# Token pairs interleaved in the stationary tiles, and weight columns streamed and written backward, in a hybrid decoder layer

## What is computed

```python
h = _rms_norm(x, attn_norm_g[l])
proj = h @ w_in[l]
...
merged = (jax.nn.sigmoid(g_da) * (o_da @ w_o_da[l])
          + jax.nn.sigmoid(g_ret) * (o_ret @ w_o_ret[l])
          + jax.nn.sigmoid(g_mem) * (o_mem @ w_o_mem[l]))
x = x + merged @ w_out[l]
hf = _rms_norm(x, ffn_norm_g[l])
x = x + (jax.nn.silu(hf @ w_ffn_gate[l]) * (hf @ w_ffn_up[l])) @ w_ffn_down[l]
```

## Time and profile before

| | |
|---|---|
| median of the runs | 1623.02 us |
| profiled execution | 1622.59 us, its span 1620.8 us |
| TensorE: matmuls | 7355, busy 1613.9 us |
| TensorE: loads of stationary values | 7355, busy 1336.1 us |
| VectorE | busy 1305.7 us |
| ScalarE | busy 915.7 us |
| GpSimd | busy 80.6 us |
| memory traffic | 341 MB, mean 211 GB/s |

### The profile page before, as it was taken

The page is one execution under the profiler, slowest core; times in us unless marked ns, Lnnn a source line. Parts: engine busy times, 40 slices in busy tenths (PEclk is TensorE's granted clock), DMA queues, the critical chain, the costliest instruction groups (busy, mean ns, idle before and its releaser), DMA issues.

```text
span 1620.8 us, 19825 instructions
## 1 busy us (share of the span) xinstructions
PE 1613.9 (100%) x7355; PEld 1336.1 (82%) x7355; DVE 1305.7 (81%) x1361; ACT 915.7 (56%) x993; POOL 80.6 (5%) x73
## 2 busy tenths in 40 slices
PE   9999999999999999999999999999999999999999
PEld 7888888888888888888888888888888888888887
DVE  5565658898677777787975589999999999999995
ACT  6654555555555544444554455665656655656653
POOL 0000000000011000000000000100100100100101
PEclk9999999999999999999999999999999999999999
DMA  9776555666645555566666746868868868868866
GB/s 351 268 214 194 157 150 177 213 201 196 193 156 168 165 162 172 180 186 202 206 233 192 258 147 210 256 211 254 243 216 245 252 206 251 246 217 240 251 213 177
DMA packets 178013, 341.45 MB, mean 211 GB/s; under 512 B 11792, under 2 KB 16400, under 8 KB 177168
## 3 DMA queue, kind: packets, MB, share of 16 engines
q1 hardware_dynamic: 167056, 319.45, 60.8%
q0 software_dynamic: 10880, 20.97, 7.1%
HBM read 317.31 MB, written 2.10 MB: 197 GB/s over the span
## 4 chain that ended last, share of the span: by engine, by line
PE 85%; issue 11%; DVE 1%; POOL 1%; DMA 1%; ACT 0%; DVEq 0%; ACTq 0%; SPq 0%; POOLq 0%
PE acc L1600 38%; PE at L1692 9%; PE at L1691 9%; PE at L1690 9%; PE acc L1692 5%; PE acc L1690 5%; PE acc L1691 5%; PE at L1600 3%; PE at L1622 2%; POOL rstd L487 1%; PE at L1653 0%; PE at L1670 0%; DMA raw<-in_w_mem_kv 0%; DMA raw<-in_w_in 0%; DVE w_lo L938 0%
## 5 line engine op out<-in xcount | busy, mean ns | idle before, releaser
L938 DVE TENSOR_TENSOR w_lo<-raw,w_hi 128x1024 fp32r<-128x1024 f32 x313 | 378.9, 1223 | 196.0 <-ACT w_hi L514 190.7
L514 ACT ACTIVATE w_hi<-raw 128x1024 fp32r<-128x1024 f32 x313 | 330.6, 1060 | 341.9 <-PE acc L1600 274.0
L1600 PE MATMUL acc<-w_hi,hT_hi 128*128 128x512 f32 x664 | 262.8, 396 | 0.0
L1600 PE MATMUL acc<-w_hi,hT_lo 128*128 128x512 f32 x664 | 258.8, 390 | 0.0
L1600 PE MATMUL acc<-w_lo,hT_hi 128*128 128x512 f32 x664 | 258.6, 390 | 0.0
L866 ACT ACTIVATE f_hi<-sum 128x2048 fp32r<-128x2048 f32 x60 | 115.3, 1922 | 122.0 <-DVE sum L1479 118.8
L1600 PE MATMUL acc<-w_hi,oT_hi 128*128 128x512 f32 x384 | 151.2, 394 | 1.1 <-DVE oT_lo L964 1.1
L1600 PE MATMUL acc<-w_hi,oT_lo 128*128 128x512 f32 x384 | 149.7, 390 | 0.0
L1600 PE MATMUL acc<-w_lo,oT_hi 128*128 128x512 f32 x384 | 149.4, 389 | 0.0
L1445 DVE TENSOR_TENSOR f_raw_rest<-f_raw,f_hi 128x2048 fp32r<-128x2048 f32 x64 | 145.3, 2284 | 4.3 <-ACT f_hi L856 4.3
L1600 PEld LDWEIGHTS acc<-w_hi,hT_hi 128*128 128x128 f32 x664 | 124.7, 188 | 27.4 <-issue 1.3
(11 more groups left out here) (348 smaller groups left out, 2858.6 us busy)
## 6 DMA issues: line engine op xcount, KB each, us to landing
raw<-in_w_in SPq DMA_DIRECT2D x208, 512.0 KB, 3.8
f_raw<-in_w_ffn_down SPq DMA_DIRECT2D x88, 512.0 KB, 5.0
f_raw<-in_w_ffn_gate SPq DMA_DIRECT2D x80, 512.0 KB, 4.0
f_raw<-in_w_ffn_up SPq DMA_DIRECT2D x80, 512.0 KB, 5.2
proj<-down POOLq DMA_DIRECT2D x40, 512.0 KB, 6.5
raw<-in_w_mem_kv SPq DMA_DIRECT2D x32, 512.0 KB, 5.7
raw<-in_w_out SPq DMA_DIRECT2D x32, 512.0 KB, 3.9
raw<-in_w_o_mem SPq DMA_DIRECT2D x16, 512.0 KB, 5.0
```

The source lines that it names most:

```text
L514: act.activation(w_hi[:, s % RING], raw[:, s % RING], ACT.Copy).then_inc(hi_done, 1)
L938: v.tensor_tensor(w_lo[:, s % RING], raw[:, s % RING], w_hi[:, s % RING].bitcast(F32), ALU.subtract).then_inc(lo_done, 1)
L1600: e = pe.matmul(dst, a[:, k0 + k, tok], w[:, s % RING, k, :], start=first and k == 0 and n == 0, stop=last and k == 1 and n == 2)
```

## The change

No instruction is added or removed, and none changes its place on its engine.

- **Interleaved tokens.** In `hT`, `aT` and the combination tiles the two token blocks lie word by word: column 2m + t holds token m of block t. A load of block t reads columns t, t + 2, ... (`t::TB`), 128 words over a span of 256. The combination tiles, before [4, 128], become [2, 128, 2], combination c at `[c // 2, :, c % 2]`. `oT` keeps its order.
- Who fills these tiles follows: the host orders the columns of `x_t` by pairs; transposes into PSUM for x and for the activations write every other word; VectorE's combinations read and write with a stride of two words.
- **Backward columns.** Every product takes the weight tile's 512 columns from last to first (`[:, ::-1]`) and writes its PSUM bank from last to first, so each result lies where it lay.

```diff
-                                            ("pad2", [P, 10 * NCOL], F32), ("cmb_hi", [P, 4, 4, P], F32R),
+                                            ("pad2", [P, 10 * NCOL], F32), ("cmb_hi", [P, 4, 2, P, 2], F32R),
...
-                    a11, a12, a21, a22 = (p_whole[:, k, t * P:(t + 1) * P] for t in range(TB) for k in range(2))
-                    v.tensor_tensor(p_mixed[:, 3], a11, a21, ALU.subtract).then_inc(p_cmb, 1)
+                    a11, a12, a21, a22 = (p_whole[:, k, t::TB] for t in range(TB) for k in range(2))
+                    v.tensor_tensor(p_mixed[:, 1, :, 1], a11, a21, ALU.subtract).then_inc(p_cmb, 1)
...
-                tok = slice(t * P, (t + 1) * P)
+                tok = slice(t, TOK, TB) if hi is hT_hi else slice(t * P, (t + 1) * P)
                 dst = acc[p][:, t, :] if p < 2 else at[:, 2 * p - 4 + t, :]
                 for n, (a, w) in enumerate(((hi, w_hi), (hi, w_lo), (lo, w_hi))):
-                    e = pe.matmul(dst, a[:, k0 + k, tok], w[:, s % RING, k, :],
+                    e = pe.matmul(dst[:, ::-1], a[:, k0 + k, tok], w[:, s % RING, k, ::-1],
                                   start=first and k == 0 and n == 0, stop=last and k == 1 and n == 2)
...
-                        e = turn(at[:, k % 4, t * P:(t + 1) * P], src[:, t, c0 + k * P:c0 + (k + 1) * P])
+                        e = turn(at[:, k % 4, t:TOK:TB], src[:, t, c0 + k * P:c0 + (k + 1) * P])
...
             def product(dst, hi, lo, whi, wlo, first, last):
 
+                dst, whi, wlo = dst[:, ::-1], whi[:, ::-1], wlo[:, ::-1]
                 pe.matmul(dst, hi, whi, start=first, stop=False)
                 pe.matmul(dst, hi, wlo, start=False, stop=False)
                 return pe.matmul(dst, lo, whi, start=False, stop=last)
 
             def block_a(t, k):
-                return hT_hi[:, k, t * P:(t + 1) * P], hT_lo[:, k, t * P:(t + 1) * P]
+                return hT_hi[:, k, t::TB], hT_lo[:, k, t::TB]
...
-                        c0 = (k % 2) * 256 + t * P
-                        e = turn(dst[:, k // 2, c0:c0 + P], gt[:, t, k * P:(k + 1) * P])
+                        c0 = (k % 2) * TOK
+                        e = turn(dst[:, k // 2, c0 + t:c0 + TOK:TB], gt[:, t, k * P:(k + 1) * P])
...
-        "x_t": inputs["x"][0].T, "mem_t": inputs["mem"][0].T,
+        "x_t": inputs["x"][0].T.reshape(D, TB, P).transpose(0, 2, 1).reshape(D, TOK), "mem_t": inputs["mem"][0].T,
```

More of the change, by code:

```diff
@@ L163, in program @@
                     for t in range(TB):
-                        for name, shape, dt in (("r_cmb", [P, 4, 4, P], F32R), ("r_sum", [P, 4, NCOL], F32R if stage else F32),
+                        for name, shape, dt in (("r_cmb", [P, 4, 2, P, 2], F32R), ("r_sum", [P, 4, NCOL], F32R if stage else F32),
                                                 ("r_hi", [P, 4, NCOL], F32R), ("r_act", [P, 2 * NCOL], F32)):
@@ L834, in _ @@
                     act.wait_ge(cmb_f, 5)
-                    act.activation(cmb_hi[:], sums[1][:].rearrange("p q (c m) -> p q c m", c=4),
+                    act.activation(cmb_hi[:], sums[1][:].rearrange("p q (a m b) -> p q a m b", a=2, b=2),
                                    ACT.Copy).then_inc(cmb_split, 1)
@@ L838, in _ @@
                     act.wait_ge(cmb_f4, 5)
-                    act.activation(cmb_hi4[:], sums[0][:, 2:4].rearrange("p q (c m) -> p q c m", c=4),
+                    act.activation(cmb_hi4[:], sums[0][:, 2:4].rearrange("p q (a m b) -> p q a m b", a=2, b=2),
                                    ACT.Copy).then_inc(cmb_split, 1)
@@ L1069, in memory_attention @@
                 if i is not None:
-                    a11, a12, a21, a22 = (p_whole[:, k, t * P:(t + 1) * P] for t in range(TB) for k in range(2))
-                    v.tensor_tensor(p_mixed[:, 3], a11, a21, ALU.subtract).then_inc(p_cmb, 1)
-                    step(v.tensor_tensor(p_mixed[:, 0], a22, a21, ALU.subtract), p_cmb, i * 5 + 3)
-                    step(v.scalar_tensor_tensor(out=p_mixed[:, 1], in0=p_mixed[:, 0], scalar=-1.0, in1=a11,
+                    a11, a12, a21, a22 = (p_whole[:, k, t::TB] for t in range(TB) for k in range(2))
+                    v.tensor_tensor(p_mixed[:, 1, :, 1], a11, a21, ALU.subtract).then_inc(p_cmb, 1)
+                    step(v.tensor_tensor(p_mixed[:, 0, :, 0], a22, a21, ALU.subtract), p_cmb, i * 5 + 3)
+                    step(v.scalar_tensor_tensor(out=p_mixed[:, 0, :, 1], in0=p_mixed[:, 0, :, 0], scalar=-1.0, in1=a11,
                                                 op0=ALU.mult, op1=ALU.subtract), p_cmb, i * 5 + 4)
-                    v.tensor_tensor(p_mixed[:, 2], a12, p_mixed[:, 1], ALU.add).then_inc(p_cmb, 1)
+                    v.tensor_tensor(p_mixed[:, 1, :, 0], a12, p_mixed[:, 0, :, 1], ALU.add).then_inc(p_cmb, 1)
                 i = head_slot(x, 6)
@@ L1315, in _ @@
                     if s == 2:
[L1316 to L1319, removed]
+                        a11, a12, a21, a22 = (r_whole[:, k, t::TB] for t in range(TB) for k in range(2))
+                        v.tensor_tensor(r_mixed[:, 1, :, 1], a11, a21, ALU.subtract).then_inc(r_cmb, 1)
+                        step(v.tensor_tensor(r_mixed[:, 0, :, 0], a22, a21, ALU.subtract), r_cmb, i * 5 + 3)
+                        step(v.scalar_tensor_tensor(out=r_mixed[:, 0, :, 1], in0=r_mixed[:, 0, :, 0], scalar=-1.0, in1=a11,
                                                     op0=ALU.mult, op1=ALU.subtract), r_cmb, i * 5 + 4)
-                        v.tensor_tensor(r_mixed[:, 2], a12, r_mixed[:, 1], ALU.add).then_inc(r_cmb, 1)
+                        v.tensor_tensor(r_mixed[:, 1, :, 0], a12, r_mixed[:, 0, :, 1], ALU.add).then_inc(r_cmb, 1)
                     if s == 6:
@@ L1428, in combine @@
                                      hT_lo[:, 2 * q0:2 * q1, :].bitcast(F32), ALU.add), done, 1)
[L1429 to L1433, removed]
+                a11, a12, a21, a22 = (pairs[:, :, k, t::TB] for t in range(TB) for k in range(2))
+                v.tensor_tensor(mixed[:, :, 1, :, 1], a11, a21, ALU.subtract).then_inc(done, 1)
+                step(v.tensor_tensor(mixed[:, :, 0, :, 0], a22, a21, ALU.subtract), done, 3)
+                step(v.scalar_tensor_tensor(out=mixed[:, :, 0, :, 1], in0=mixed[:, :, 0, :, 0], scalar=-1.0, in1=a11, op0=ALU.mult,
                                             op1=ALU.subtract), done, 4)
-                step(v.tensor_tensor(mixed[:, :, 2], a12, mixed[:, :, 1], ALU.add), done, 5)
-            mixed4 = sums[1][:].rearrange("p q (c m) -> p q c m", c=4)
+                step(v.tensor_tensor(mixed[:, :, 1, :, 0], a12, mixed[:, :, 0, :, 1], ALU.add), done, 5)
+            mixed4 = sums[1][:].rearrange("p q (a m b) -> p q a m b", a=2, b=2)
             last = sums[0][:, 0:2].rearrange("p q (k c) -> p q k c", k=2)
-            mixed1 = sums[0][:, 2:4].rearrange("p q (c m) -> p q c m", c=4)
+            mixed1 = sums[0][:, 2:4].rearrange("p q (a m b) -> p q a m b", a=2, b=2)
             def low_whole(f, p, u):
@@ L1717, in combined @@
                 def combined(c):
-                    return p_cmb_hi[:, i, c, :], p_cmb_lo[:, i, c, :]
+                    return p_cmb_hi[:, i, c // 2, :, c % 2], p_cmb_lo[:, i, c // 2, :, c % 2]
                 pe.wait_ge(lo_done, g + 2)
@@ L1847, in combined @@
                 def combined(c):
-                    return r_cmb_hi[:, i, c, :], r_cmb_lo[:, i, c, :]
+                    return r_cmb_hi[:, i, c // 2, :, c % 2], r_cmb_lo[:, i, c // 2, :, c % 2]
                 pe.wait_ge(lo_done, g + 2)
@@ L1923, in combined @@
             def combined(i, c):
-                return cmb_hi[:, i, c, :] if i < 4 else cmb_hi4[:, i - 4, c, :], cmb_lo[:, i, c, :]
+                hi = cmb_hi[:, i] if i < 4 else cmb_hi4[:, i - 4]
+                return hi[:, c // 2, :, c % 2], cmb_lo[:, i, c // 2, :, c % 2]
             def plain(f, p, u, first, last):
@@ L1960, in down_half @@
                 for k in range(4):
-                    e = product(at[:, 2 * (n % 2) + t, :], hi[:, k, t * P:(t + 1) * P],
-                                lo[:, k, t * P:(t + 1) * P], *whole(f, p, u, k), k == 0, k == 3)
+                    e = product(at[:, 2 * (n % 2) + t, :], hi[:, k, t::TB], lo[:, k, t::TB], *whole(f, p, u, k),
+                                k == 0, k == 3)
                 return e
```

10 lines of the change are left out of this document (5 added, 5 removed).

## The result

The changed kernel takes 1664.92 us (two runs, 1664.81 and 1665.04) against 1623.02: a ratio of 1.0258, 95% interval 1.0214 to 1.0302. It is slower. The forecast was 1568 us with a range of 1550 to 1655, so the time lies outside the range and on the other side.

The account below looks back on a forecast made before the run. TensorE's matmul spacing, not waits, was taken as the bound. Savings of 31.0 less 0.3, 23.4 and 1.0 us, together 55, take the span from 1620.8 to 1565.8; with time around the span 1568 us, range 1550 to 1655.

Parts of the forecast that it names:

- part 2 of the change: Reversed moving and output columns in all 6771 products: 216 ns for the 5427 also interleaved, 226.7 unchanged for the other 1344.
- The 1344 on `oT`: Products on the not interleaved tile, with reversal alone: spacing taken as unchanged at 226.7 ns.
- The upper bound: Slowest product spacing allowed for reversed columns: the surcharge doubles, 226.7 + 13.4 = 240.1 ns.
- The stride of the load: Interleaved stationary tiles: loads take at most twice 0.11 us, hidden behind the product before, so cost 0.
- Rival C: Strided load disturbs the stream more: 5427 interleaved products grow 10.7 to 13.4 ns, 1681 to 1696 us; chance 0.20.
- Rival B: Surcharge belongs to the float32r product itself; order and stride leave spacing at 226.7 ns, 1623 us; chance 0.22.
- the weaker row: Product at 423.28 us with no load beside it until 0.32 us later, yet its record is 0.39 us like others.
- Rival D: Reversed columns halve the PSUM write rate: every product at least 427 ns, about 2975 us; chance 0.02.
- The other costs taken at nothing: 120 transposes writing every other PSUM word (at most 12 us), VectorE's strided combinations (at most 4 us), host layout: each 0.
- VectorE as the next bound of the chunk: In the FFN, VectorE would end the chunk at 59.5 us, not TensorE's 59.2, saving 2.6 us, not 2.9.
- 0.56: Chance of rival A, the forecast itself: the surcharge goes where both edits act, 1568 us, own range 1550 to 1595.

Follow-up runs that it names:

- e4: Separate matmul-only program, not the layer: 48 products per line, load or stream shifted by words; stream 8 words on 233.1 to 233.3 ns, both 8 on 227.7.
- e5: Kernel before plus an unused 8-word tile behind `hT_lo`, moving later tiles 32 bytes on, no access pattern changed: 1643.57 us against 1621.88, ratio 1.0133.
- e7: Separate matmul-only program: smaller loads, more shifts, other widths, bf16 and float32; a one-column load 231.0 ns, eight columns 226.7, reversed with eight 233.3.
- e3: Separate matmul-only program, 96 matmuls per access pattern: plain 226.7 ns, weights reversed 233.4, PSUM reversed 226.8, strided load 233.3, bf16 216.0.
- e2: Kernel before with only the weight and PSUM columns reversed, tokens in blocks: 1664.11 us, ratio 1.0254.
- e8: Separate program, 48 float32r products per line, shifts of reversed and strided patterns: reversed 233.3 to 236.9 ns, strided alone 230.0 to 235.0.
- e1: Changed kernel with weight and PSUM columns forward again, only the tokens interleaved: 1656.35 us, ratio 1.0205.
- e6: Kernel before with only the PSUM columns written backward, weights streamed forward: 1622.13 us, ratio 1.0001.

## Why the prediction was wrong, and where it was right

- **What bounds the kernel: right.** No wait, the spacing of the matmuls, 6771 products. The result follows from that count: 6771 x 6.67 = 45.1 us, of which 42.2 are seen.
- **The step that failed** is in part 2 of the change: "I take 216 for the 5427 products where both edits act, since the phase-dependent row says the surcharge is not a constant of the instruction". The row said that the spacing depends on more than the instruction, and e4 and e5 bear that out. But it had it one way only: 230 in an unsettled stretch against 226.7 in a settled one. It showed a surcharge that can grow, and no row showed one that shrinks. The 216 came from float32 matmuls, which carry no such surcharge in any of the three patterns of e7: it was another kind of instruction and no value that this one was seen to reach. Measured in its place: 233.3 where both edits act, 6.67 ns more instead of 10.7 less.
- **A misreading under that step.** "Eight float32 matmuls of 256 columns (lines 1653, 1670) take 1.73 us, 216 ns each" counts records. Each of these lines issues four matmuls in such a group, and e7 shows two records for one. A matmul of 256 columns takes about 432 ns, almost four times per column what a product takes and not twice. If the array's time per record is 213.3 ns, as the prediction had it, the 216 is half of an instruction and the surcharge per matmul about 5 ns, an estimate. bf16, at 216.0 ns for one record of 512 columns, is the closer comparison, and that came only with e3.
- **The 1344 on `oT`** were taken at 226.7 under reversal alone. They went to 233.3, and e2 shows it for all products. 1344 x 6.67 = 9.0 us of the 42.
- **The upper bound** of 240.1 held: the kernel has 233.3, and the dearest line of e3, e4 and e8 that has only the patterns of the change took 236.9.
- **The stride of the load** was put at nothing, since twice 0.11 us would stay hidden. e1 has the stride without the reversal, and it costs 1656.35 against 1622.64 us. The load's record grew only to 193 or 194 ns there, well inside the spacing, so the time wasn't lost by waiting for a longer load; the spacing of the products itself grew. In the whole change the reversal alone already costs as much, so this term can't be read from the total. The 0.11 us itself doesn't add up with its row either: one load and one product are 0.34 us, and the earlier trace rows has 0.31.
- **Rival C had the right side.** Its sentence that the settled state "is the best that the present pattern reaches, and a new pattern may settle in a worse one" is what happened. Its size was off: it gave 10.7 to 13.4 ns, against 6.67 measured, and 1681 to 1696 us. It also left the `oT` products alone. Its mechanism, a load that meets the stream more often, isn't borne out: reversed products with a load of eight columns still take 233.3 (e7), a shift without any stride costs as much (e5), and the reversal alone costs the same with the loads as they were (e2). Its "against", that the load has time enough, was right and had no bearing.
- **Rival B** said that the surcharge belongs to the product and not to the load beside it., which the prediction called the weaker row, pointed there, and e7 agrees so far that at 512 columns a smaller load doesn't make the product shorter. But B took it from there that no pattern could touch it, and that was wrong.
- **Rival D** (reversed columns in PSUM) fell: e6, 1622.13 us. The Trainium skill, "Advanced Engine Details and Errata", section Memory Cachelines, asks that every two consecutive elements in PSUM be contiguous; a backward bank still does that, and the measurement agrees with this reading of it. The transposes that now write every other word of PSUM don't do that, and they kept 109 ns; there the measurement doesn't bear the rule out.
- **The same section on SBUF**, that two hits on a 16-byte line are enough, was cited for the load, "by it the load is free". The load record grew from 188 to 197 ns and stayed within the spacing, but the product beside a strided load takes 233.3 ns (e1), so the stride wasn't free. And a stream with a stride of two words, which also has two hits on each line, takes 453 ns a product (e8, L106) instead of 226.7. Here the page and the measurement differ, and the measurement decides.
- **The other costs taken at nothing** were right: the 120 transposes with a stride in PSUM keep 109 ns; VectorE's combinations brought no wait. VectorE as the next bound of the chunk didn't come into play, since TensorE got slower and not faster.
- **The chances**: 0.56 stood on a step that had no row for its direction. Weighed by the rows, "can shrink" and "can grow" had the same evidence at best, and the one difference there was (230 against 226.7) was for "can grow".

Shown: each edit alone takes a product of 512 columns from 226.7 to 233.3 ns; in the kernel they don't add up; a backward bank in PSUM and the other engines have no part; a smaller load removes neither the surcharge nor the price of the reversal; shifting one tile by 32 bytes costs as much as either edit. What stays open: by what mechanism float32r pays while bf16 and float32 don't, why it comes in these steps, why the reversal costs nothing at 256 columns, why two edits cost no more than one, and why shifts of 28 and 64 words cost nothing and others do. A stream of products with no load between them wasn't tried, so it isn't shown that the load must be there for the surcharge.

## What to carry to other kernels

A kernel whose TensorE never waits is worth the spacing of its matmuls and nothing else: divide the chain's long pieces by their counts, for each data type and each tile apart, before and after, and check in the code that a record is one instruction. A row in which the same instruction is sometimes slower shows that it can get slower; to bet on faster, look for a row of the same instruction that is faster. And where float32r products run at their best spacing, leave the stationary and moving tiles contiguous, forward and at their places: a pad of 32 bytes cost this kernel 1.3%.

## What the runs showed of the hardware

- A float32r product of 512 columns, with a load of 128 columns before it and tiles placed as in the kernel before, takes 226.67 ns from start to start at 2.4 GHz, 13.3 over the array's 213.3; bf16 takes 216.0. With 256 and 384 columns of float32r it is 119.8 and 173.3, 13.1 and 13.3 over; with 504 columns 16.7 over.
- A float32 matmul shows as two records: 48 matmuls of 256 columns are 96 records of 215.8 ns, 431.7 ns a matmul.
- Backward reading of the moving tile, a stride in the stationary one, or a start shifted by 8 words against the other tile each take it to 233.3. Together they stay there, or go to at most 236.9. At 256 columns backward reading costs nothing (118.3 against 119.8), and in bf16 and float32 neither it nor the stride does.
- Both tiles shifted alike by 8 words give 227.7, one shifted by 64 words 226.7 to 227.3, the stream shifted by 28 words 226.7.
- Writing PSUM from last column to first is free (1622.13 us against 1621.88 beside it).
- A moving tile read at every other word takes 453 ns a product, and in blocks of 16 words from two halves 240 ns.
